# A two-block transformer in one fp32 kernel: one 128-column block per expert, and the norm ahead of the first router

## The reference, cut to what matters

```python
lat = lat + mod_l[2] * y_l
h_l = rms_norm_2(lat, norm2_w[layer]) * (1.0 + mod_l[4]) + mod_l[3]
lat = lat + mod_l[5] * expert_choice_ffn(h_l, moe_router[layer], moe_w_gate[layer], ...)

def expert_choice_ffn(h, router_w, w_gate, w_up, w_down):
    cap = EC_CAPACITY * n // N_EXPERTS        # 64 tokens (latent), 32 (context)
    aff = jax.nn.softmax((h @ router_w).astype(F32), axis=-1)
    gate, idx = lax.top_k(jnp.swapaxes(aff, 1, 2), cap)
    xe = jax.vmap(lambda hb, ib: hb[ib])(h, idx)
    a = jnp.einsum('becd,edf->becf', xe, w_gate)
    u = jnp.einsum('becd,edf->becf', xe, w_up)
    ye = jnp.einsum('becf,efd->becd', jax.nn.silu(a) * u, w_down) * gate[..., None]
    return ...  # the 16 results added back at their tokens
```

## Time and profile before

| | us |
|---|---|
| median of three runs | 3525.95 (3524.45 to 3527.00) |
| the profiled execution | 3526.57 |
| its span | 3524.8 |

### The profile page before, as it was taken

The page is one execution under the profiler, slowest core; times in us unless marked ns, Lnnn a source line. Parts: engine busy times, 40 slices in busy tenths (PEclk is TensorE's granted clock), DMA queues, the critical chain, the costliest instruction groups (busy, mean ns, idle before and its releaser), DMA issues.

```text
span 3524.8 us, 34008 instructions
## 1 busy us (share of the span) xinstructions
PE 3327.5 (94%) x14077; PEld 1524.8 (43%) x14077; DVE 1152.7 (33%) x2215; ACT 671.2 (19%) x1435; POOL 14.8 (0%) x20
## 2 busy tenths in 40 slices
PE   8999889999988999898999999999999999899998
PEld 3444444344444344355856433333334654433332
DVE  1111461211156244574564212121224571211112
ACT  1000350100045020112123211111011362111111
POOL 0000000000000000000000000000000000000000
PEclk9999999999999999999999999999999999899999
DMA  4333201233320121210421577777781101699996
GB/s 176 125 142 143 96 1 67 92 127 130 143 96 13 72 76 72 81 42 13 152 77 49 216 310 287 286 286 285 298 325 56 48 1 56 278 421 420 420 420 276
DMA packets 85452, 588.09 MB, mean 167 GB/s; under 512 B 10217, under 2 KB 11404, under 8 KB 15029
## 3 DMA queue, kind: packets, MB, share of 16 engines
q1 hardware_dynamic: 79776, 575.70, 40.7%
q10 hardware_dynamic: 5524, 10.22, 0.9%
HBM read 583.79 MB, written 2.10 MB: 166 GB/s over the span
## 4 chain that ended last, share of the span: by engine, by line
PE 88%; DVE 8%; ACT 3%; issue 1%; DMA 0%; ACTq 0%; another core or an unknown queue 0%; SPq 0%; POOL 0%; DVEq 0%; PEldq 0%
PE ps L492 14%; PE ps L1102 7%; PE ps L2197 6%; PE ps L2256 6%; PE ps L840 5%; PE ps L489 5%; PE ps L2127 4%; PE ps L2291 3%; PE ps L2275 3%; PE ps L2109 3%; PE ps L2529 2%; PE ps L2213 2%; PE ps L2305 2%; PE ps L2040 2%; PE ps L2225 2%; PE ps L1437 2%
## 5 line engine op out<-in xcount | busy, mean ns | idle before, releaser
L492 PE MATMUL ps<-mem 128*128 128x512 f32 x1152 | 505.8, 598 | 1.9 <-DVE mem L614 1.9
L492 PEld LDWEIGHTS ps<-mem 128*128 128x128 f32 x1152 | 218.8, 191 | 284.5 <-issue 282.4
L2169 DVE SCALAR_TENSOR_TENSOR mem<-ps,mem 128x512 f32<-128x512 f32 x128 | 96.0, 750 | 570.4 <-PE ps L2127 564.5
L1102 PE MATMUL ps<-mem 128*128 128x512 f32 (+1 forms) x768 | 254.0, 493 | 0.9 <-ACT mem L944 0.9
L2197 PE MATMUL ps<-mem 128*64 128x512 f32 x1024 | 232.3, 597 | 0.9 <-ACT mem L2145 0.9
L2256 PE MATMUL ps<-mem 128*64 128x512 f32 x1024 | 230.1, 597 | 0.7 <-ACT mem L2151 0.7
L1102 PEld LDWEIGHTS ps<-mem 128*128 128x128 f32 x768 | 147.9, 193 | 107.5 <-issue 95.7
L840 PE MATMUL ps<-mem 128*128 128x512 f32 x384 | 169.9, 597 | 1.8 <-DVEq L160 1.8
L489 PE MATMUL ps<-mem 128*128 128x512 f32 x384 | 167.0, 594 | 0.0
L557 ACT ACTIVATE mem<-ps 128x512 f32<-128x512 f32 x48 | 28.7, 598 | 682.6 <-PE ps L492 682.6
L2127 PE MATMUL ps<-mem 128*128 128x512 f32 x256 | 136.0, 622 | 1.9 <-ACT mem L2156 1.4
(11 more groups left out here) (365 smaller groups left out, 3961.5 us busy)
## 6 DMA issues: line engine op xcount, KB each, us to landing
mem<-in_moe_w SPq DMA_DIRECT2D x384, 1024.0 KB, 11.0
mem<-in_w_in SPq DMA_DIRECT2D x48, 1024.0 KB, 9.6
mem<-in_ada_w SPq DMA_DIRECT2D x48, 1024.0 KB, 6.8
mem<-in_hy_w_in SPq DMA_DIRECT2D x24, 1024.0 KB, 6.6
mem<-in_w_out SPq DMA_DIRECT2D x12, 1024.0 KB, 9.0
mem<-in_k_win_l SPq DMA_DIRECT2D x8, 1024.0 KB, 6.9
mem<-in_hy_w_out SPq DMA_DIRECT2D x8, 1024.0 KB, 4.9
mem<-in_sw_w_in SPq DMA_DIRECT2D x6, 1024.0 KB, 7.0
```

Source lines behind the costliest of these rows:

```text
L492: m = mm(ps[:, j % 4, :], Wc[s][:, k, t * P:(t + 1) * P], HTL[:, k, :], start=(k == 0), stop=(k == KD - 1))
L1102: m = mm(ps[:, j % 4, 0:L], Wc[s][:, k, (j % 4) * P:(j % 4 + 1) * P], H[:, k, :], start=(k == 0), stop=(k == KD - 1))
L2169: stt(XT[:, j, :], ps[:, bank, :], mod(m_.layer, 5, j, 0), XT[:, j, :], ALU.mult, ALU.add)\
```

## The change

In `Moe`, the layout of buffers and banks, and the plan of the jobs. `GU` gets two buffers and `G` one, the turned values stay in the bank of their pair, three banks (layer 0) or five (layer 1) serve the jobs, and each expert has two spots, (e, 0) and (e, 1). The router's weights and the iota row get room of their own, are loaded at the start of the first gate instead of a phase earlier (the same two DMAs, by ACT's queue), and layer 0 has no shift after a gather any more.

```diff
-            for dst, src in ((v(SC_, KD * 32), a["router"][0]), (v(LS_, CAP_L), a["k_iota"])):
-                A.e.dma_start(dst, src).then_inc(S["const_in"], 16)
...
-        G_, GU_, AT_ = hg.take(2 * 512), hg.take(512), hg.take(KD * CAP_L)
+        G_, GU_, AT_ = hg.take(512), hg.take(2 * 512), hg.take(KD * CAP_L)
...
-                s.GU = v(GU_, 512)
+                s.GU = [v(GU_ + i * 512, 512) for i in range(2)]
                 s.GUC = v(GUC_, 512)
-                s.G = [v(G_ + i * 512, 512) for i in range(2)]
+                s.G = v(G_, 512)
...
+            def shift(s, k, n):
+                return 0.0 if s.ctx else mod(s.layer, 3, k, n)
...
-                inner = (3,) if s.ctx else (3, 4, 5, 6)
+                inner = (2, 3, 6) if s.ctx else (2, 3, 4, 5, 6)
...
+                    more = group + 1 < N_GROUP
+                    ys = [("y", pair - 1, 4 * (e % 2) + k) for k in range(4)] if pair else []
+                    ahead = [("x", group + 1, i)] if more else ys[:2]
+                    after = ys if more else ys[2:]
+                    if s.ctx and more:
+                        after.insert(len(after) // 2, ("xc", group + 1, i))
+                    if s.ctx and group:
+                        after.append(("yc", group - 1, i))
                     if e % 2:
-                        s.put((e, 5, 0), inner, "g", pair)
-                    if s.ctx and group:
-                        s.put((e, 5, 1), inner, "yc", group - 1, i)
+                        after.append(("g", pair, 0))
                     if s.ctx and i == GROUP - 1:
-                        s.put((e, 5, 1), inner, "gc", group)
+                        after.append(("gc", group, 0))
+                    for job in ahead:
+                        s.put((e, 0), inner, *job)
+                    for job in after:
+                        s.put((e, 1), inner, *job)
```

```diff
+            def lat(e, kh):
+                for pair in range(2):
+                    w = [Wh[st.get_half(2 * pair + x)] for x in range(2)]
+                    if e and kh == 0:
+                        A.e.wait_ge(S["c_ready"], 2 * (e - 1) + pair + 1)
+                    for k in range(4 * kh, 4 * kh + 4):
+                        for x in range(2):
+                            m = mm(ps[64 * x:64 * x + 64, pair, :], m_.XS[e // GROUP % 2][:, k, e % GROUP, 0:CAP_L],
+                                   w[x][:, k % 4, :], start=(k == 0), stop=(k == KD - 1))
+                            if kh and k == 4 and pair == 0 and x == 1:
+                                m.then_inc(S["w_used"], 4)
+                    if kh:
+                        m.then_inc(A.mark("psum_full"), 1)
+
+            def cxt(e, kh):
+                w = [Wh[st.get_half(i)] for i in range(4)]
+                if e and kh == 0:
+                    A.e.wait_ge(S["ctx_hidden"], e)
+                for k in range(4 * kh, 4 * kh + 4):
+                    for i in range(4):
+                        m = mm(ps[32 * i:32 * i + CAP_C, 4, :], m_.XS[e // GROUP % 2][:, k, e % GROUP, CAP_L:],
+                               w[i][:, k % 4, :], start=(k == 0), stop=(k == KD - 1))
+                        if e and k == 0 and i == 3:
+                            m.then_inc(S["w_used"], 4)
+                if kh:
+                    m.then_inc(A.mark("ctx_full"), 1)
...
+                cxt(e, 0)
+                lat(e, 0)
+                st.next(4)
+                lat(e, 1)
+                cxt(e, 1)
+                st.next(4)
+                pe_turn(A, m_, e, 0)
                 pe_turn(A, m_, e, 1)
-                pe_aux(A, m_, (e, 3, 1))
+                pe_aux(A, m_, (e, 0))
+                pe_turn_ctx(A, m_, e)
+                pe_aux(A, m_, (e, 1))
                 w = []
                 if e:
                     A.e.wait_ge(S["e_ready"], e)
```

```diff
+                    if e:
+                        A.e.wait_ge(S["c_ready"], 2 * (e - 1) + pair + 1)
                     for kh in range(2):
                         w = [Wh[st.get_half(x)] for x in range(2)]
...
+                    m.then_inc(A.mark("psum_full"), 1)
+                pe_turn(A, m_, e, 0)
+                pe_aux(A, m_, (e, 0))
+                pe_turn(A, m_, e, 1)
+                pe_aux(A, m_, (e, 1))
...
+                for kh in range(2):
+                    w = [Wh[st.get_half(x)] for x in range(2)]
+                    A.e.wait_ge(S["c_ready"], 2 * e + kh + 1)
...
+                            if k == 4 * kh and x == 1:
+                                m.then_inc(S["w_used"], 2)
...
-                A.e.wait_ge(S["c_ready"], 2 * e + pair)
             for k in range(4):
-                m = tr(ps[:, 2, k * P:(k + 1) * P], m_.GU[:, k * P:(k + 1) * P], IDENT)
+                m = tr(ps[:, pair, k * P:(k + 1) * P], m_.GU[pair][:, k * P:(k + 1) * P], IDENT)
...
+                if e:
+                    A.e.wait_ge(S["turned"], 2 * (e - 1) + pair + 1)
+                act(m_.GU[pair], ps[:, pair, :], ACT.Copy).then_inc(A.mark("act_out"), 1)
...
@@ -2368,29 +2495,22 @@
...
                 copy(e, 0)
...
-                act_aux(A, m_, (e, 2, 0))
+                copy(e, 1)
                 silu(e, 0)
-                act_aux(A, m_, (e, 2, 1))
-                act_aux(A, m_, (e, 3, 0))
-                copy(e, 1)
-                act_aux(A, m_, (e, 3, 1))
-                silu(e, 1)
-                act_aux(A, m_, (e, 4, 0))
-                act_aux(A, m_, (e, 4, 1))
                 if m_.ctx:
+                    silu(e, 1)
+                    act_aux(A, m_, (e, 0))
                     silu_ctx(e)
+                else:
+                    act_aux(A, m_, (e, 0))
+                    silu(e, 1)
+                act_aux(A, m_, (e, 1))
```

```diff
+            def router(z, L, H, bank):
+                for k in range(KD):
+                    A.e.wait_ge(S["h_ready"], z * KD + k + 1)
+                    r = 32 * (k % 4)
+                    m = mm(ps[r:r + 32, bank, 0:L], m_.RTR[:, k, :], H[:, k, :], start=(k < 4), stop=(k >= 4))
+                m.then_inc(A.mark("f_ready"), 1)
...
+            chunk(0)
+            pe_norm(A, m_.SQ(T), m_.RS(T), T, 7, 1)
+            chunk(1, 0, 4)
+            A.e.wait_ge(S["inverted"], 1)
+            pe_spread(A, m_.RS(T), T, GATE_SPREAD, P)
+            chunk(1, 4)
+            chunk(2)
+            chunk(3)
+            A.e.wait_ge(S["const_in"], 32)
+            router(0, T, HL, 3)
+            chunk(4)
+            logits_turn(0, T, 0, 6)
+            chunk(5)
+            shares_turn(0, T, 0, 7)
+            chunk(6)
+            chunk(7)
+            ctx_sums(range(6))
+            token_rows(HL, tokens[0:2])
+            ctx_sums((6, 7)).then_inc(A.mark("stat"), 1)
+            token_rows(HL, tokens[2:4])
+            A.e.wait_ge(S["inverted"], 2)
+            pe_spread(A, m_.RSC, TC, (1, 2))
+            token_rows(HL, tokens[4:])
+            router(1, TC, HC, 0)
+            token_rows(HC, ctokens)
+            logits_turn(1, TC, 4, 1)
+            slots_turn(0, T, 0, 6)
+            shares_turn(1, TC, 4, 2)
+            A.e.wait_ge(S["selected"], 4)
...
+            def scaled(z, X, H, parts):
+                A.e.wait_ge(S["spread"], z + 1)
+                for k in range(KD):
+                    stt(blocks(H[:, k, :]), blocks(X[:, k, :]), gains[z][:, k:k + 1], parts, ALU.mult, ALU.mult)\
+                        .then_inc(A.mark("scaled"), 1)
...
+            dve_squares(A, XT, m_.SQ(T))
+            gain(0)
+            gain(1)
+            invert(0, m_.RS(T))
+            scaled(0, XT, HL, spread(GATE_SPREAD, P))
+            logits(0, 4, 0, 6)
+            shares(0, 4, 0)
+            dve_top(A, m_, 0, S["g_ready"], 1, "c_ready", lambda: invert(1, m_.RSC),
+                    lambda: scaled(1, CT, HC, spread((1, 2))))
+            logits(1, 2, 4, 1)
+            A.e.wait_ge(S["const_in"], 32)
+            select(0, 4, 0, 6)
+            shares(1, 2, 4)
             dve_top(A, m_, 1, S["g_ready"], 2, "c_ready")
-            dve_gate_select(A, m_, 1, 1)
+            select(1, 2, 4, 3)
```

More of the change, by code:

```diff
@@ new lines, in router, with logits_turn @@
+            def router(z, L, H, bank):
[4 more added lines that the diff above has]
+                m.then_inc(A.mark("f_ready"), 1)
+            def logits_turn(z, L, t0, bank):
+                A.e.wait_ge(S["act_out"], z + 1)
+                for t in range(L // P):
+                    m = tr(ps[:, bank, t * P:(t + 1) * P], m_.LOGITS[:, (t0 + t) * P:(t0 + t + 1) * P], IDENT)
+                m.then_inc(A.mark("scores"), 1)
@@ new lines, in pe_first_gate @@
+            tokens = [(t, half) for t in range(T // P) for half in range(2)]
+            ctokens = [(t, half) for t in range(TC // P) for half in range(2)]
+            chunk(0)
[8 more added lines that the diff above has]
+            router(0, T, HL, 3)
@@ L1962, in pe_first_gate @@
             end_phase(A)
+        GATE_SPREAD = (4, 5, 6, 7)
+        CTX_TMP = [v(SEL_ + 4096 + 256 * i, 256) for i in range(4)]
```

(33 more changed lines are left out.)

311 lines of the change are left out of this document (127 added, 184 removed).

## The result

The changed kernel takes 3554.95 us (median of 3 runs, 3550.21 to 3555.5) against 3525.95: a ratio of 1.0072, 95% interval 1.0058 to 1.0087. It is slower by 29 us on the medians and by 23.6 on the two profiled executions (3526.57 and 3550.21). The forecast was 3556.

A forecast was written before the change was run, and what follows sets the result against it. PE bounds layer 0's experts, PE and the weight stream layer 1's, a PE, ACT and DVE chain the first gate. Layer 0 +44 (-34 + 53 + 25), layer 1 -9, gate -5: +30 on 3526.57, 3556 us; range 3545 to 3568.

The forecast's parts named there:

- PE's work in layer 0: Layer 0's experts: PE's work falls from 681.75 to 648 us, 34 us less, bounds 28 to 38.
- The stands: Layer 0, before cxt(e, 0): PE waits 3.5 us (2.8 to 4.2) for weights at 15 of 16 experts, 53 us.
- The clock: Layer 0: 3.4 us of half clock behind nearly each wait at cxt(e, 0), costing 1.7 each, 25 us (0 to 50).
- Rival 1: Layer 0: waits of 2.8 to 4.2 us come but the clock holds; +10 us, 3537 us; chance 0.2.
- rival 2: Layer 0: the clock stays low longer, two stretches behind each wait; +25 us more, 3581 us; chance 0.13.
- The second quad: Layer 0, lat(e, 1): waits 0 to 1 us per expert for its other two halves, hidden by the slower first quad.
- Layer 1: Layer 1's experts: weights set the end, first issue 3.65 us earlier; -9 us, bounds 0 to -14.
- Gate: First gate: turns go, norm moves ahead of the router, nothing follows the gathers; -5 us, bounds -9 and +4.
- The step on which the sign hung: Layer 0: next expert's first quad complete after 14.0 us, down quad lasts only 10.5, so PE waits 3.5 us.

The follow-up runs named there:

- early-release kernel: Changed kernel with the second gate and up quad's buffer reported free at turn 0's first transpose, not the first down product: 3482.61 us, ratio 0.9871.
- the first three experiments: Each on the changed kernel: buffer released a block earlier, 3482.61 us; lat(e, 0) ahead of cxt(e, 0), 3491.89 us; three extra matmuls before cxt(e, 0), 3524.83 us.
- the later release: Changed kernel with the second gate and up quad's buffer reported free 3.5 us later, at the ninth pair of down products: 3611.25 us, ratio 1.0236.
- The filled stand: Changed kernel with three extra matmuls ahead of cxt(e, 0)'s wait for weights, from the second expert on: 3524.83 us, ratio 0.9993.
- latent first: Changed kernel with lat(e, 0) ahead of cxt(e, 0) in layer 0's experts, the second quad's release still late: 3491.89 us, ratio 0.9901.
- gate alone: Kernel before with only the changed first gate (norm ahead of the router, loads on ACT's queue, factor's turns gone): 3522.0 us, ratio 0.9987.

## Why the prediction was right

The mechanism is the forecast one, and the runs show each of its parts. That the median of 3554.95 lies 1 us from 3556 is luck. The sum was built on the profiled executions, and there it gave +30 where +23.6 came; the profiled execution of the changed kernel is the fastest of its three. Within the stage of layer 0 the errors partly cancel too. Step by step, with the sums over the 16 experts taken from the starts of PE's runs:

- **PE's work in layer 0, forecast -34 (bounds 28 to 38): -38.3.** The stage without stands, low clock and waits is 643.4 us (643.0 in the early-release kernel), not 648. The costs at changes of width that I left in were too many: a "y" in the block takes 0.86, not 0.89, leaving the block costs nothing beyond its runs (0.2 per expert in the forecast), and the three turns take 1.37 per expert, not 1.47. The value lies just past the end of my bounds. Of the 38.3, 10 were idle in the kernel before.
- **The stands, forecast +53: +55** by the starts (the waits show 52.3). `cxt(e, 0)` begins 13.6 to 15.8 us behind the first down product, mean 14.15, less the 10.48 that the down products take. The mean hides two kinds: nine stands are of 3.1 to 3.3 us, with landings at the near end of the rows, and six, with late landings, of 3.7 to 5.4. The one value of 3.5 met their mean, not either kind. Release, order and landing each did their part as the forecast had it: the first three experiments and the later release move the stand as their arithmetic says.
- **The clock, forecast +25: +21.3** in `cxt(e, 0)`. Twelve of the 15 stands bring a low stretch; it adds 1.3 to 2.8 us to the 32 matmuls behind them, since the low stretch begins inside the idle in some. The filled stand shows that the idle, and not the narrow matmuls, is the cause of these. Rival 1 (the clock holds) is refuted, rival 2 (two stretches behind each stand) too: only three of the 15, the longest, had 6.83 us at 0.50, twice the 3.41 of the others.
- **The second quad, forecast 0 to 1 us per expert, hidden by the slow first one: 2.3 us in all.** Once the clock holds it shows: 7 to 9 us in the filled and the early-release kernels.
- **Layer 1, forecast -9: -9.5.** The mechanism (weights set the end) is right: from the first issue to the last landing it takes 448.1 us where 447.9 was forecast, and the first issue comes 3.8 us earlier in the stage. Where the waits stand is not: I had about 1 us at each expert, and all 12 come from 3362.9 on, in a stage that lasts from 3069.6 to 3529.3. The likely reason, that the ring of 15 halves starts full and is drained slowly, was not tested.
- **Gate, forecast -5: -5.6.** The steps came where they were placed. In the forecast's times (3.9 us later than the changed kernel's own) DVE's top starts at 1908.5 and the gathers run from 1938.4 to 1954.2. How near the size came is in part luck: of the eight traces with this gate two take 79.7 to 79.9 us for the stretch, this one among them, and six take 76.4 to 76.5, which is 9.0 to 9.1 less than before; they lose 5.1 us to low clock and not 8.5. What I had not placed is an idle of PE among the turns of the latent rows, with the clock at 0.50 from 1920.2 to 1930.4:

```profile
1924.32 1.97 PE L1942 MATMUL ps<-mem 128*128 128x128 f32 x8 [5.51 <-ACT mem L2068]
```

The step on which the sign hung was the comparison of 14.0 us with the 10.5 of the down quad. The Trainium skill's price for a load (DMA: Bandwidth & Descriptors, Anatomy of one DMA), by which I estimate that the quad would have been there 11.6 us after its first issue, would have made the stand 2.2 us; the trace has at least 12.2 from the first issue (13.34 from the first down product, less 1.12), and the rows were the better guide. The Trainium skill's limit of about 3 us for an idle (TensorE: Matmul & The Clock Gate, Why this matters for your kernels) is too generous for these traces: the clock fell behind idles of 2.42 us, 2.83 us (latent first) and 1.56 us (gate alone).

## What to carry to other kernels

Before work is gathered into one block, ask what that work was hiding: here it stood among the weight-bound stretches and gave each load its time. When an order changes, go through every "buffer free" signal and move it to the last reader of the new order; one increment moved by a block of 10 us was worth 70 us. Where weights are wanted in full, start with the consumer that needs the fewest of them. And an order in blocks needs banks enough: the jobs that ran unbroken on three waited for each other on one.

## What was not expected of the hardware

- The length of an idle alone doesn't decide on the clock. Behind 2.96 us (at 2084.41) it was 0.50, behind 2.95 us (at 2364.87) it stayed 1.00. Of the nine stands of 2.93 to 3.08 us six brought a low stretch and three didn't; all six of 3.51 to 5.18 us did. In front of a "gc" 1.55 us left the clock at 1.00 in the kernel before, and 1.56 us in the gate-only kernel didn't.
- Three useless matmuls (2.84 us) in each stand made the stage 25.4 us shorter: 21.3 of it is the clock, the rest the steadier landings less longer waits of `lat`.
- SP's issue of a 1 MB load takes 0.33 to 0.43 us in the chain shown, and up to 1.44 (at 2398.83 in the changed kernel); so the same four issues spread over 2 us or over 3.4.
